# Matrix-memory heads: memory products in strips of 32 tokens, eight memory buffers, attention inside the o product

## The reference, cut to what matters

```python
s = q @ k.T * exp(d - m_t)
num = w_inter * (q @ C) + s @ v
den = w_inter * (q @ n) + sum(s)
h = num / maximum(abs(den), exp(-m_t))
C_new = decay_prev * C + (w_k * k).T @ v
n_new = decay_prev * n + sum(w_k * k)
```

## Time and profile before

| | |
|---|---|
| median of 3 runs | 2731.1 us (2729.4 to 2731.57) |
| profiled execution: span from first to last instruction | 2730.8 us |
| TensorE busy | 2631.1 us, 96% of the span |
| VectorE, ScalarE, GpSimd busy | 1405.0, 1004.8, 222.7 us |
| mean granted TensorE clock | 0.985 |
| moved by DMA | 389.77 MB, 143 GB/s |

### The profile page before, as it was taken

The page is one execution under the profiler, slowest core; times in us unless marked ns, Lnnn a source line. Parts: engine busy times, 40 slices in busy tenths (PEclk is TensorE's granted clock), DMA queues, the critical chain, the costliest instruction groups (busy, mean ns, idle before and its releaser), DMA issues. The chain is left out here.

```text
span 2730.8 us, 44822 instructions
## 1 busy us (share of the span) xinstructions
PE 2631.1 (96%) x16761; PEld 2523.8 (92%) x16761; DVE 1405.0 (51%) x2094; ACT 1004.8 (37%) x1345; POOL 222.7 (8%) x306
## 2 busy tenths in 40 slices
PE   7999999999999999999999997599999999999998
PEld 5969789797999999999999997599999999999997
DVE  5444444444754454454445446965455454554545
ACT  4323333233443332333333336244343342333435
POOL 1110201102200000000000003610000000000002
PEclk9999999999999999999999998799999999999999
DMA  4545445454344444444444434144444444444443
GB/s 137 163 153 164 164 124 166 156 163 162 125 143 149 144 140 141 140 140 133 151 144 133 147 128 134 48 142 149 153 144 151 149 147 149 146 149 148 141 141 108
DMA packets 224748, 389.77 MB, mean 143 GB/s; under 512 B 25829, under 2 KB 53045, under 8 KB 223965
## 3 DMA queue, kind: packets, MB, share of 16 engines
q1 hardware_dynamic: 222511, 382.93, 44.0%
q10 hardware_dynamic: 2045, 4.00, 0.4%
HBM read 363.40 MB, written 23.43 MB: 142 GB/s over the span
## 5 line engine op out<-in xcount | busy, mean ns | idle before, releaser
L1019 DVE TENSOR_TENSOR w_lo<-w_raw,w_hi 128x1024 fp32r<-128x1024 f32 x664 | 815.9, 1235 | 1043.8 <-ACT w_hi L759 1041.5
L759 ACT ACTIVATE w_hi<-w_raw 128x1024 fp32r<-128x1024 f32 x664 | 699.0, 1058 | 1364.6 <-PE bank L419 1328.8
L417 PE MATMUL bank<-xh,w_hi 128*128 128x336 f32 (+2 forms) x3584 | 1135.6, 317 | 49.6 <-issue 23.2
L418 PE MATMUL bank<-xl,w_hi 128*128 128x336 f32 (+2 forms) x3584 | 1129.7, 315 | 0.0
L419 PE MATMUL bank<-xh,w_lo 128*128 128x336 f32 (+2 forms) x3584 | 1127.4, 315 | 0.0
L417 PEld LDWEIGHTS bank<-xh,w_hi 128*128 128x128 f32 x3584 | 676.7, 189 | 58.5 <-issue 44.9
L419 PEld LDWEIGHTS bank<-xh,w_lo 128*128 128x128 f32 x3584 | 678.5, 189 | 0.0
L418 PEld LDWEIGHTS bank<-xl,w_hi 128*128 128x128 f32 x3584 | 677.7, 189 | 0.3
L417 PE MATMUL bank<-hh,w_hi 128*128 128x336 f32 (+1 forms) x1632 | 511.7, 314 | 4.5 <-issue 4.5
L419 PE MATMUL bank<-hh,w_lo 128*128 128x336 f32 (+1 forms) x1632 | 511.4, 313 | 0.0
L418 PE MATMUL bank<-hl,w_hi 128*128 128x336 f32 (+1 forms) x1632 | 511.3, 313 | 0.0
(11 more groups left out here) (247 smaller groups left out, 1257.4 us busy)
## 6 DMA issues: line engine op xcount, KB each, us to landing
w_raw<-in_w_up SPq DMA_DIRECT2D x640, 256.0 KB, 2.8
w_raw<-in_w_down SPq DMA_DIRECT2D x336, 256.0 KB, 3.4
w_raw<-in_w_mlstm_in SPq DMA_DIRECT2D x192, 256.0 KB, 3.1
area<-in_state_mlstm_C SPq DMA_DIRECT2D x32, 512.0 KB, 5.3
w_raw<-in_w_mlstm_out SPq DMA_DIRECT2D x64, 256.0 KB, 3.0
out_C_sample<-area SPq DMA_DIRECT2D x32, 512.0 KB, 3.0
w_raw<-in_w_up SPq DMA_DIRECT2D x64, 192.0 KB, 2.5
w_raw<-in_w_pool SPq DMA_DIRECT2D x16, 256.0 KB, 3.1
```

The source lines that it names most:

```text
L417: pe.matmul(out, wh, xhk, start=first, stop=False)
L418: pe.matmul(out, wh, xlk, start=False, stop=False)
L759: nc.scalar.activation(w_hi[:, s], w_raw[:, s], ACT.Copy).then_inc(hi_done, 1)
L1019: V.tensor_tensor(w_lo[:, s], w_raw[:, s], w_hi[:, s].bitcast(F32), ALU.subtract).then_inc(lo_done, 1)
```

## The change

The sample tokens are laid out in four strips of 32 columns or partitions: each holds two samples (8 + 8 tokens) in its upper half; the first strip's lower half holds the prompt's last 16 tokens. `qk` and `v` get 384 columns (TA), evacuated in two instructions (272 prompt columns, 64 strided sample columns). C has eight buffers, one for each sample. The new memories are made by f32 products of 32 contraction rows, one strip each, with weighted keys for two samples at a time, so the split parts and their work on ACT, POOL and DVE go. The numerators with the old C have 32 output partitions, one strip each. Attention is cut into pieces that stand inside the o product (which goes to SA instead of SB), the new memories inside the next head's q, k product, for head 3 inside the first MLP product. DVE's updates and SP's stores move with them. Sigmoid is taken tile by tile. `acc` and `rt` become `sums`; the clearing at the start is split, and the part for which the gate weights wait no longer waits for the transposes.

```diff
+TA = 3 * 128
+STRIPS, PER = 4, 2
-        Cr = view(11584, 4 * 2 * DV).rearrange("p (s k n) -> p s k n", s=4, k=2)
+        Cr = [view(at, 2 * DV).rearrange("p (k n) -> p k n", k=2)
+              for at in [0] + [8614 + i * 2 * DV for i in range(6)] + [15526]]
...
+            def c_loads(h, batch):
+                for b in batch:
+                    if b == 0:
+                        wait_apart(sp, sp_passed, kt_ready, h + 1)
+                        wait_apart(sp, sp_passed, qm_ready, h + 1)
+                    elif not isinstance(h, int):
+                        sp.wait_ge(c_stored[b], 16 * h)
...
+                        if not isinstance(h, int):
+                            if (blk, k) == (0, 2):
+                                c_stores(h - 1, 0)
+                            if (blk, k) == (0, 5):
+                                c_stores(h - 1, 1)
+                        if (blk, k) == (0, 6):
...
+                            c_loads(h, (2, 4, 6))
+                        if (blk, k) == (1, 0):
+                            c_loads(h, (1, 3, 5, 7))
+                        if (blk, k) == (1, 2):
+                            c_loads(h, (0,))
...
+            def new_states(h, e):
+
+                def products(r):
+                    i, k = r // 2, r % 2
+                    if r == 0:
+                        pe.wait_ge(evac, e)
+                        pe.wait_ge(wkb_ready, h + 1)
+                    else:
+                        pe.wait_ge(c_updated, 16 * h + 4 * r)
+                    for s in range(STRIPS):
+                        own = slice(32 * s, 32 * s + 32)
+                        pe.matmul(SB[s][:, :], wkb[own, i, k * P:(k + 1) * P], vtok[own, 2, :],
+                                  start=True, stop=True).then_inc(cnew_ready, 1)
+
+                return {at: (lambda r=r: products(r)) for r, at in enumerate((1, 2, 4, 5))}
...
+                gemm(SA, c, 0, KT, 4, xh, xl, 0, free=None if first else after(e - 8),
+                     amid={5: stabilisers} if first else {**new_states(h - 1, e), 7: stabilisers})
...
+                def past_numerators():
+
+                    for b in range(NB):
+                        pe.wait_ge(c_landed[b], 16 * (h + 1))
+                    for i in range(PER):
+                        for k in range(2):
+                            for s in range(STRIPS):
+                                b = PER * s + i
+                                pe.matmul(SB[2][32 * s:32 * s + 32, :], qm[:, k, b, :], Cr[b][:, k, :],
+                                          start=False, stop=False, skip_group_check=True)
+                    pe.matmul(SB[2][:, :], PS2, vtok[:, 2, :], start=False, stop=True).then_inc(num_ready, 1)
+                    pe.wait_ge(den_read, h + 1)
...
+                def hidden():
+
+                    pe.wait_ge(n_read, h + 1)
+                    pe.wait_ge(hn_ready, 3 * h + 3)
...
-                gemm(SB, c, 16, KT, 4, xh, xl, 0, free=after(e + 4), amid={3: values})
+                gemm(SA, c, 16, KT, 4, xh, xl, 0,
+                     guard={0: (ps_ready, h + 1), 1: (ktok_ready, h + 1)},
+                     amid={1: values, 3: own_numerators, 4: past_numerators, 7: hidden})
+
+                for k in range(2):
                     pe.wait_ge(wkp_ready, h + 1)
+                    pe.wait_ge(evac, e + (8 + (1, 4)[k]))
...
+                    if first and q == 0 and i == 0:
+                        amid = {**new_states(H - 1, e), 7: history}
...
+                for f in (2, 0, 1, 3):
+                    V.tensor_tensor(o[:, f], SA[f][:, 0:T], rbc[:, :], ALU.mult).then_inc(evac, 1)
...
+            def update(h, c, k0):
+
+                for r in range(4):
+                    i, k = r // 2, r % 2
+                    for s in range(STRIPS):
+                        b = PER * s + i
+                        dve.wait_ge(cnew_ready, 16 * h + (4 * r + s + 1))
+                        V.scalar_tensor_tensor(Cr[b][:, k], Cr[b][:, k], WI[:, NS * b + NS - 1:NS * b + NS],
+                                               SB[s][:, :], ALU.mult, ALU.add).then_inc(c_updated, 1)
+                    los(c, k0 + (4, 5, 7, 8)[r], k0 + (5, 7, 8, 9)[r])
...
+            G.memset(area[:, 14758:15526], 0.0).then_inc(consts, 1)
             pool.wait_ge(st_tr, 16)
-            G.memset(area[:, 6528:9216], 0.0).then_inc(consts, 1)
+            G.memset(area[:, 5184:6496], 0.0)
+            G.memset(area[:, 0:3072], 0.0).then_inc(cleared, 1)
```

More of the change, by code:

```diff
@@ L184, in program @@
         ntok = view(6784, DK, NB * H)
[L185 to L188, removed]
+        wgr = view(8614, KT * 8).rearrange("p (k n) -> p k n", n=8)
+        wgg = view(8742, KT * 36).rearrange("p (k n) -> p k n", n=36)
+        sqr = view(9318, 4 * T).rearrange("p (s n) -> p s n", n=T)
+        row = [view(10662 + i * T, T, 36) for i in range(12)]
+        rpad = [view(7528 + i * P, P, H) for i in range(2)]
         E = view(0, 4 * GW).rearrange("p (f t) -> p f t", t=GW)
@@ L310, in _, with c_stores @@
                          I["state_mlstm_m"].rearrange("a b h -> a (b h)").to_broadcast([P, NB * H])).then_inc(in_gate, 16)
[L312 to L317, removed]
+            def c_loads(h, batch):
[5 more added lines that the diff above has]
+                        sp.wait_ge(c_stored[b], 16 * h)
+                    src = I["state_mlstm_C"][0, b].rearrange("h (k p) v -> p (h k) v", p=P)
+                    sp.dma_start(Cr[b], src[:, bass.ds(2 * h, 2), :]).then_inc(c_landed[b], 16)
+            def c_stores(h, i):
+                for b in range(i, NB, PER):
+                    sp.wait_ge(c_updated, 16 * h + 8 * (i + 1))
+                    sp.dma_start(O["C_sample"][0][b].rearrange("h (k p) v -> p (h k) v", p=P)[:, bass.ds(2 * h, 2), :],
+                                 Cr[b]).then_inc(c_stored[b], 16)
             def head(h, c):
@@ L404, in _ @@
             sp.wait_ge(stored, 16 * (2 + 2 + 12))
-            for s in range(4):
-                sp.wait_ge(c_stored[s], 2 * H * 16)
+            for b in range(NB):
+                sp.wait_ge(c_stored[b], H * 16)
             sp.wait_ge(cst_stored, 16 * H)
@@ L483, in sum_squares @@
                 pe.wait_ge(ssq_ready, k)
[L484 removed]
+                pe.matmul(out, ones[:, :], sums[k], start=True, stop=True).then_inc(rms_mm, 1)
+            def new_states(h, e):
[11 more added lines that the diff above has]
+                return {at: (lambda r=r: products(r)) for r, at in enumerate((1, 2, 4, 5))}
             def head(h, c, e):
@@ L1076, in _ @@
             step(V.tensor_tensor_scan(mrow[:, :], row[10][h4], row[4][h4], 0.0, ALU.add, ALU.max))
-            V.tensor_tensor(mtrow[:, :], row[7][h4], mrow[:, :], ALU.add).then_inc(rows_ready, 1)
+            step(V.tensor_tensor(mtrow[:, :], row[7][h4], mrow[:, :], ALU.add))
+            for to, src in ((rpad[0], row[8][h4]), (rpad[1], mtrow[:, :])):
+                V.tensor_copy(to[:, 0:META], src[:, 2 * P:NP])
+                m_ = V.tensor_copy(owned(to), owned(src[:, NP:], 16))
+            m_.then_inc(rows_ready, 1)
             def head(h, c, e):
@@ L1203, in ffn @@
                 for q in range(nq):
-                    los(c, k0 + 4, k0 + 11)
+                    if first and q == 0 and i == 0:
+                        update(H - 1, c, k0)
+                        dve.wait_ge(c_stored[0], 16 * H)
+                        V.memset(E[:, :, 0:2], 0.0).then_inc(e_zero, 1)
+                        los(c, k0 + 9, k0 + 11)
+                    else:
+                        los(c, k0 + 4, k0 + 11)
                     if first and q == 0:
@@ new lines, in head @@
+                pool.wait_ge(qm_ready, h + 1)
+                ends = X[:, X2:XW].rearrange("p (s c) -> p s c", c=32)[:, :, META + NS - 1:32:NS]
+                part = wsum[:, 0:4].rearrange("p (s i) -> p s i", i=PER)
+                G.tensor_tensor(part, ends[:, 0:2], ends[:, 2:4], ALU.add).then_inc(wsum_ready, 1)
+                wait_apart(pool, pool_passed, wsum_ready, 2 * h + 1)
+                G.tensor_tensor(wsum[:, 4:6], wsum[:, 0:2], wsum[:, 2:4], ALU.add).then_inc(wsum_ready, 1)
+                wait_apart(pool, pool_passed, wsum_ready, 2 * h + 2)
@@ L1433, in _ @@
             sum_of_squares(1)
-            for b in range(4):
-                pool.wait_ge(c_stored[b], 2 * H * 16)
+            for b in range(NB):
+                pool.wait_ge(c_stored[b], H * 16)
             pool.wait_ge(cst_stored, 16 * H)
```

450 lines of the change are left out of this document (216 added, 234 removed).

## The result

The kernel after takes **2658.3 us** (median of 4 runs, 2657.9 to 2659.6) where the kernel before took 2731.2 beside it: a ratio of 0.9734 [0.972, 0.9747], 72.9 us less. The forecast was 2700, so the direction was right and the size was not: the gain is more than twice the 31 us forecast, 0.3 us above the lower end of the range, and within 6 us of the rival "full overlap" (2664).

What follows compares the result with a forecast made beforehand. TensorE, busy 96% of the span, was taken to bound the kernel by work, not waiting. Terms: -110.1 + 29.2 + 34.4 + 6.4 + 3.4 + 0.6 + 7.5 - 2.2 = -30.8, so 2700.0 us; range 2658 to 2735.

Steps and rivals of the forecast that it cites:

- full overlap: Rival for the strip products: strips take records from their own queues, four products cost 0.86 us; 2664 us, chance 0.23.
- The step that failed: Strip products in the heads: records keep program order, two share each 0.43 us; 7.3 us a head for old memories.
- past numerators: Products with the old memories in each head: 17 x 0.43 = 7.3 us a head, bounds 3.4 and 13.8.
- new memories: Four groups of four strip products a head: 2.15 us a group, 8.6 us a head, bounds 3.4 and 13.8.
- Changes of shape: Five strip groups a head, entered and left: ten changes of 0.16 us, 1.6 us a head, 6.4 in all.
- cuts: Attention inside weight products: seven more cuts a head, 0.12 us each on the first record behind, 3.4 us in all.
- Padding: 48 padded columns of the last score product and its two k: 0.6 us in all.
- Waits on DVE: New memories waiting for DVE: 2.3 us at three head starts, 3.4 and 1.8 at first FFN pass; 7.5 together.
- Hidden work: DVE, ACT and POOL work moved beside TensorE, including hn chain, normalisers and out product's low parts: hidden; C transfers zero.
- Start: Gate weights no longer wait for the zeroing of 2,688 columns: -2.2 us.
- No overlap: Rival for the strip products: partial strips run one after another, 27.5 us a head; 2746.5 us, chance 0.15.
- The wait on memory transfers: Rival in SP's queue: weights behind waits for stores, C loads behind weights; 6 us a head lost, 2724, chance 0.12.

Runs made afterwards that it cites:

- strip by strip: Kernel after with the past numerators' loops turned, all four products of one strip standing before the next strip's: 2679.6 us, ratio 0.9816.
- the run with 15668: Kernel after with the sums of squares from the third on at column 15668 instead of 15670: 2662.7 us, ratio 0.975.
- the run behind the o product: Kernel after with own numerators, past numerators and hn transposes put behind the o product instead of inside it: 2680.7 us, ratio 0.9824.
- the two runs of 8 bytes: Sums of squares from the third on: kernel before, in the large area at column 15350, 2728.7 us; kernel after, at 15668 instead of 15670, 2662.7 us.
- after once more: Kernel after, unchanged, profiled a second time; no time of its own is given for this profile.
- two by two: Kernel after with the past numerators' loops turned, two products of each strip in a row, then again: 2657.7 us, ratio 0.9736.
- one column strip: Kernel after with all sixteen products of the past numerators written to output partitions 0 to 31: 2698.8 us, ratio 0.9885.

## Why the prediction was right and wrong

**The step that failed** is the one that priced the strips: "If a strip must be free and order is kept, the second record of strip s waits 0.43 us for the first, and the first of strip s + 1 can start beside it, no earlier." Order is not kept between strips. Each strip has a queue of its own, in which up to three records were seen to wait; the second record waits there, and the next strip starts at once. In the sum this is the term "past numerators", forecast 7.3 us a head and measured 3.58, and "new memories", forecast 8.6 and measured 4 x 1.07 = 4.3. Together 32 of the 43.5 us by which the sum (30.8) fell short of the spans (74.3). The argument rested on rows in which records start in program order, but no two of those products lie in different strips; nothing in them could show the order between strips. The working named that gap, bounded it rightly (3.4 to 13.8) and then chose the value by an analogy with those rows. That the range still holds the result, by 0.3 us, is luck: its lower end was drawn from full overlap with the other terms as forecast, and those came out lower as well.

The Trainium skill, page "TensorE: Matmul & The Clock Gate", Part 3, would have been nearer: its 3.07 times for four row strips became 60.0 / 18.2 = 3.3 here (one by one, with its clock, against overlapped), and its 2.38 times for three column strips became 55.7 / 14.6 = 3.8 with four. The rule of the same part that matmuls start in strict program order, which the working set beside its own reading, does not hold for these products: in the run strip by strip the first product of strip 1 started at 1.75 us and the fourth product of strip 0, which stands ahead of it, at 2.60.

The other terms, in the order of the sum:

- *Changes of shape*, 6.4 forecast, and *cuts*, 3.4: they are one cost, 7.4 in all. A group of past numerators takes 3.58 us where eight times 0.43 make 3.44, a group of new memories 1.07 where twice make 0.86; these 0.14 and 0.21, 3.9 us in all, are already in the 3.58 and 1.07. Beside them a group of strips starts 0.25 us after the last weight record instead of 0.154, and behind new memories the first weight record takes 0.26: 20 x 0.093 + 16 x 0.104 = 3.5. The other eight of the 28 cuts, by products of the full array, cost nothing: the denominators start 0.15 us after the last weight record like any weight record. The price of a cut was read from a place where the stabilisers cut in, a product of 4 rows, and was taken for all.

```profile
121.84 0.32 PE L440 MATMUL bank<-xh,w_lo 128*128 128x336 f32 x1
...
131.64 0.32 PE L440 MATMUL bank<-xh,w_lo 128*128 128x336 f32 x1
...
194.91 0.42 PE L438 MATMUL bank<-xh,w_hi 128*128 128x336 f32 x1
195.17 0.32 PE L439 MATMUL bank<-xl,w_hi 128*128 128x336 f32 x1
```

- *Padding*, 0.6 forecast: 2.2. The forecast had the scores alone. Of the denominators' eight products five had 80 output columns and now have 128: 1.70 us a head (121.99 to 123.69) instead of 1.30 (142.16 to 143.46), 1.6 in all.
- *Waits on DVE*, 7.5 forecast: 0.46 at one head start of three, 1.76 at the first FFN pass, 0.2 at its second group, and 1.5 by the clock, so 3.9; where the clock stays at 1.00 the second group waits 1.6 and the sum is about the same. At the FFN pass the places were right, and so was the size at the second group where the clock stayed; the first wait was 1.76 instead of 3.4: the adds began 3.8 us behind the out product's end (635.81 to 639.62) instead of the 5.3 that the earlier trace rows led to, because each of the three x_low groups ahead of them took 4.06 us instead of 4.59. POOL's additions run beside these, and the run with 15668 shows what they do to x_low (below).
- *Hidden work*: the hn chain, the normalisers, the out product's low parts and C's transfers cost TensorE nothing, as forecast; that the first of these is hidden by its place alone, the run behind the o product shows (22.4 us).
- *Start*, -2.2 forecast: -0.67 in this trace, and not to be told from the spread of identical starts.
- *Not in the sum*: POOL's additions, 3.2 and 4.3 us by the traces of the two runs of 8 bytes.

DVE in order of time, for that point: the last x_low and adds at the first FFN pass of after, then eight x_low beside the fourth sum in after and in the run with 15668:

```profile
633.36 4.06 DVE L1057 SCALAR_TENSOR_TENSOR xl<-x,par,xh 128x336 fp32r<-128x336 f32 x4
637.35 2.35 DVE L1048 TENSOR_TENSOR w_lo<-w_raw,w_hi 128x1024 fp32r<-128x1024 f32 x2
639.62 1.74 DVE L1067 TENSOR_TENSOR x<-bank,x 128x336 f32<-128x336 f32 x4
...
1700.14 7.71 DVE L1057 SCALAR_TENSOR_TENSOR xl<-x,par,xh 128x322 fp32r<-128x322 f32 x8
```
```profile
1701.10 8.79 DVE L1057 SCALAR_TENSOR_TENSOR xl<-x,par,xh 128x322 fp32r<-128x322 f32 x8
```

The slower addition on POOL slows DVE's work beside it by 1.1 us in eight. That the shorter x_low at the first FFN pass has the same cause is likely, since the second sum stands at an equal place (14758) there, but no run moved that one.

With the measured values the sum up to the first tails is -110.1 + 14.3 + 17.2 + 3.5 + 2.2 + 3.9 - 0.7 = -69.7, against -69.2 by the marks. Behind them 3.2 to 4.3 of 5.1 us are accounted for; the rest was not traced.

**The rivals.** Full overlap is what happened; its mechanism was in the text, with 0.23. No overlap decides the sign, as forecast: 2755.7 when it is forced. The wait on memory transfers did not come: TensorE waits for no C, and for a weight chunk 0.2 us once in the whole program.

## What to carry to other kernels

Small products that use a quarter of the array's rows or columns are worth placing in different strips, four in a row; here that alone turned a change 25 us slower than its predecessor into one 73 us faster. The order in which they are issued need not alternate at every product, but no strip may be fed more than two f32 products (four records) before the others get theirs. And before a rule about order is drawn from a trace, look whether any row in it could have shown the opposite.

## What the runs showed of the hardware that was not expected

- Each strip holds three waiting records of its own (or one whole f32 product behind the one that runs): with eight records for one strip in a row the next strip started 1.75 us late (beside the fifth), with four in a row 0.01 us late.
- An accumulator moved by 8 bytes changed an f32 addition of 336 columns on POOL from 1070 to 940 ns, and DVE's x_low beside it from 8.79 to 7.71 us in eight. Which multiple counts, and whether the accumulator's place counts by itself or against the other operand's, was not tried beyond these columns.
- Products one by one on 32 rows were followed by 3.4 us at half the granted clock in the next head's weight product (0.53 from 205.5 to 208.9 us) though TensorE waited for nothing; overlapped, the same products left it at 1.00. A wait of 3.9 us a head (the run behind the o product) had such a sequel in all four heads and cost 1.6 times what the list of waits says (5.6 + 0.6 us a head). The wait of 1.8 us at the first FFN pass had it in two traces (after and the run behind the o product) and not in five others with the overlap kept there (after once more, strip by strip, two by two, one column strip, 15668).
- A cut into a stream of products costs by the change of shape: 0.09 us on entering strips and 0.10 on the first record behind them, nothing for products of the full array.
